# A parallel pooling and attention layer on one core: factoring the first half's norm out of x, and projecting keys and values together

## What is computed

```python
for layer in range(DEPTH):                       # DEPTH = 1, 16 meta frames + 1024 frames, D_MODEL = 2048
    hn = _rmsnorm(h, norm_g[layer])              # each frame divided by its rms, times norm_g
    proj = hn @ w_in[layer]                      # 2048 x 4352
    pv, pg, q, k, v, ag = jnp.split(proj, SPLITS, axis=-1)
    pool_out = _multiscale_pool(pv, pool_w[layer], pool_scale[layer])   # trailing means over 2, 4, 8, 16 frames
    attn_out = _attention_branch(q, k, v, q_norm_g[layer], k_norm_g[layer], sinks[layer])
    mixed = jnp.concatenate([jax.nn.silu(pg) * pool_out, jax.nn.silu(ag) * attn_out], axis=-1)
    h = h + mixed @ w_out[layer]
return h[:, N_META:]
```

## Time and profile before

| | |
|---|---|
| median of 3 runs | 1263.39 us (1261.69 to 1263.98) |
| profiled execution | 1263.45 us, span 1261.8 us |
| TensorE busy | 1239.5 us, 98% of the span |
| VectorE busy | 896.2 us, 71% |
| ScalarE busy | 635.4 us, 50% |
| POOL busy | 68.6 us, 5% |
| HBM read, written | 125.14 MB, 8.39 MB |

### The profile page before, as it was taken

The page is one execution under the profiler, slowest core; times in us unless marked ns, Lnnn a source line. Parts: engine busy times, 40 slices in busy tenths (PEclk is TensorE's granted clock), DMA queues, the critical chain, the costliest instruction groups (busy, mean ns, idle before and its releaser), DMA issues.

```text
span 1261.8 us, 19307 instructions
## 1 busy us (share of the span) xinstructions
PE 1239.5 (98%) x6200; PEld 1042.5 (83%) x6200; DVE 896.2 (71%) x1425; ACT 635.4 (50%) x1490; POOL 68.6 (5%) x78
## 2 busy tenths in 40 slices
PE   4999999999999999999999999999999999999998
PEld 4988898898988987888888888888888888788887
DVE  6557786888879886665644677788798887854553
ACT  6434456465563654544533344655646556444442
POOL 0000000010010110000000000000101103000000
PEclk9999999999999999999999999999999999999999
DMA  5232333222332225544533333222322222343442
GB/s 211 83 92 78 96 96 85 84 77 67 101 92 78 73 67 206 188 137 147 189 126 91 91 94 88 83 82 86 98 72 88 75 92 88 112 133 125 166 142 84
DMA packets 70609, 134.38 MB, mean 106 GB/s; under 512 B 8064, under 2 KB 10240, under 8 KB 69888
## 3 DMA queue, kind: packets, MB, share of 16 engines
q1 hardware_dynamic: 68160, 125.17, 31.6%
q0 software_dynamic: 2384, 8.39, 1.9%
HBM read 125.14 MB, written 8.39 MB: 106 GB/s over the span
## 4 chain that ended last, share of the span: by engine, by line
PE 94%; DVE 3%; DMA 1%; ACT 1%; issue 1%; SPq 0%; ACTq 0%
PE R L1059 19%; PE R L1060 18%; PE R L1063 18%; PE S L1282 4%; PE S L1283 4%; PE S L1281 4%; PE OP L1283 2%; PE OP L1281 2%; PE R L1282 2%; PE OP L1282 2%; PE R L1283 2%; PE R L1281 2%; PE OP L1060 1%; PE OP L1063 1%; PE OP L1059 1%; PE OP L1207 1%
## 5 line engine op out<-in xcount | busy, mean ns | idle before, releaser
L430 ACT ACTIVATE wh<-raw 128x512 fp32r<-128x512 f32 x400 | 250.4, 631 | 494.4 <-PE R L1063 269.8
L725 DVE TENSOR_TENSOR wl<-raw,wh 128x512 fp32r<-128x512 f32 x400 | 282.1, 708 | 241.7 <-ACT wh L430 240.5
L1059 PE MATMUL R<-act_h,wh 128*128 128x512 f32 (+1 forms) x1168 | 426.2, 370 | 0.0
L1060 PE MATMUL R<-act_l,wh 128*128 128x512 f32 (+1 forms) x1168 | 422.5, 367 | 0.0
L1063 PE MATMUL R<-act_h,wl 128*128 128x512 f32 (+1 forms) x1168 | 403.2, 365 | 0.0
L1059 PEld LDWEIGHTS R<-act_h,wh 128*128 128x128 f32 x1168 | 220.1, 188 | 36.9 <-DVE wl L725 0.8
L1060 PEld LDWEIGHTS R<-act_l,wh 128*128 128x128 f32 x1168 | 220.0, 188 | 34.7
L1063 PEld LDWEIGHTS R<-act_h,wl 128*128 128x128 f32 x1168 | 210.5, 188 | 36.8
L949 DVE RECIPROCAL scr<-scr 128x512 f32<-128x512 f32 x32 | 107.3, 3353 | 1.1
L402 POOL TENSOR_TENSOR scr<-scr 128x527 f32<-128x527 f32 (+3 forms) x40 | 50.6, 1265 | 799.2 <-ACT pv_last L430 364.4
L430 ACT ACTIVATE pm<-OP 16x128 fp32r<-16x128 f32 x256 | 68.3, 267 | 5.4
(11 more groups left out here) (206 smaller groups left out, 1825.0 us busy)
## 6 DMA issues: line engine op xcount, KB each, us to landing
raw<-w_in_blocks SPq DMA_DIRECT2D x272, 256.0 KB, 2.6
raw<-w_out_in SPq DMA_DIRECT2D x128, 256.0 KB, 3.0
scr<-xcat SPq DMA_DIRECT2D x32, 256.0 KB, 4.3
mixed<-xcat SPq DMA_DIRECT2D x4, 1024.0 KB, 8.3
res<-xcat SPq DMA_DIRECT2D x16, 256.0 KB, 3.2
out<-scr POOLq DMA_DIRECT2D x14, 256.0 KB, 2.6
out<-res POOLq DMA_DIRECT2D x14, 256.0 KB, 4.9
scr<-pool_w_in SPq DMA_DIRECT2D x8, 256.0 KB, 3.2
```

What stands on the lines that cost most here:

```text
L430: return nc.scalar.activation(dst, src, ACT.Copy)
L725: return nc.vector.tensor_tensor(dst, a, b, ALU.subtract)
L1059: mm(o, wh[:, b, w], act_h[:, k, c], start=(k == 0), stop=False)
L1060: mm(o, wh[:, b, w], act_l[:, k, c], start=False, stop=False)
```

## The change

Half one: x is transposed as it is, and each frame's factor is applied when a product leaves PSUM. For that, the factors are laid out in columns (`r_columns`), transposed by TensorE after query block 0 (`r_transposes`), and copied to a row buffer `rb` that all partitions hold (`r_rows`). All products now leave PSUM through VectorE (`scaled`): times `rb` in half one, times 1.0 in half two. That holds for queries (`q_out`), keys and values (`kv_out`), gates (`gate_in`) and pooled values (`pv_out`, formerly ScalarE's). ScalarE squares queries and keys from SBUF. The gate is now x (1 + tanh(x/2)), with the factor 0.5 put into `o_out` and `hscale` (`gate_tanh`, `gate_out`). The sums of squares of x come after the splits of x, four passes between weight splits. x is loaded in five column pieces, weight blocks between them. Keys and values are projected block by block in turn (`first_tiles`), in both halves. The steps of a query tile move: the copy out stands where the square stood, remainder and sums of squares one step later, root and `q_norm` one step later as well. `QB` and the waits on banks follow.

```diff
-FIRST_SPLITS = {2: 2, 5: 3, 7: 4, 11: 5, 15: 6}
+FIRST_SPLITS = {0: (0,), 3: (1, 2), 7: (3, 4), 11: (5, 6), 15: (7,)}
+FIRST_LOADS = ((0, 2), (2, 4), (4, 8), (8, 12), (12, 16))
...
+        QB = [S[:, 0, :]] + [(R[1][:, :], R[0][:, :], O)[t % 3] for t in range(PAIRS - 1)]
+        YB = [R[0][:, :], S[:, 0, :], S[:, 1, :], O]
...
+            def first_frames(i):
+                k0, k1 = FIRST_LOADS[i]
...
+            def first_block(n, free=True):
+                load_block(n, n % RAW, w_in[TILE_BLKS * (n % 2) + n // 2, :, :], free)
+            sp.dma_start(cst[:, 0:P], consts[:, 0:P]).then_inc(s_id, 16)
+            sp.dma_start(x_meta, xcat[0:META, :]).then_inc(s_xmeta, 16)
+            first_frames(0)
+            sp.dma_start(vec[:, :], vecs).then_inc(s_vec, 16)
+            first_block(0, free=False)
+            first_frames(1)
+            first_block(1, free=False)
+            first_frames(2)
+            first_block(2, free=False)
+            first_block(3, free=False)
+            first_frames(3)
+            sp.dma_start(cst[:, P:C_N], consts[:, P:C_N]).then_inc(s_cst, 16)
+            first_frames(4)
...
-            act.wait_ge(s_init, 5)
-            for n in range(RAW):
-                split_high(0, n)
...
+            def first_stats(r):
+                stats(x_first[r], P, r, r, r)
...
+                for off in FIRST_SPLITS.get(k, ()):
+                    split_high(0, off)
...
+            first_stats(0)
+            first_stats(1)
+            act.wait_ge(s_init, 5)
...
+                for s in range(5 if h == 0 else 0, KV_BLKS):
                     split_high(h4, s + LEAD)
+                    if h == 0 and s < 7:
+                        first_stats(s - 3)
...
+                def r_columns():
+                    act.wait_ge(s_xrs, 2)
+                    for r in range(ROWT):
+                        copy(r_col[:, r, :], xrs[:, r:r + 1].to_broadcast([P, P])).then_inc(s_rc, 1)
+                    copy(r_meta, xrs[0:META, ROWT:ROWT + 1].to_broadcast([META, P])).then_inc(s_rc, 1)
+                def r_rows():
+                    act.wait_ge(s_rt, 1)
+                    copy(rb[:, META:COLS], PT[:, :]).then_inc(s_rb, 1)
+                    copy(rb[:, 0:META], PM[:, 0:META]).then_inc(s_rb, 1)
...
                 def q_square(t):
-                    product_done(act, h, KV_BLKS + t * TILE_BLKS)
+                    act.wait_ge(s_qv, h * PAIRS + t + 1)
                     if t >= 2:
                         act.wait_ge(s_qss, h * PAIRS + t - 1)
                     for dst in (q_sq[t % 2], q_sqh[t % 2]):
-                        nc.scalar.activation(dst, QB[t % 4][:, :], ACT.Square).then_inc(s_qsq, 1)
+                        nc.scalar.activation(dst, mixed[:, PAIRS + t, :], ACT.Square).then_inc(s_qsq, 1)
...
                 for s in range(Q_BLKS + 1):
+                    if s < Q_BLKS:
+                        split_high(h4 + KV_BLKS // RAW, s + LEAD)
+                    if s == 1 and h == 0:
+                        r_rows()
+                    if s == 2:
+                        k_square()
+                    if s == 4:
+                        k_sqrt()
                     if s and s % 4 == 0:
                         q_square(s // 4 - 1)
-                    if s < Q_BLKS:
-                        split_high(h4 + KV_BLKS // RAW, s + LEAD)
-                    if s > 4 and s % 4 == 1:
+                    if s > 4 and s % 4 == 2:
                         q_sqrt(s // 4 - 1)
...
-                    def gate_exp(n, bank):
-                        product_done(act, h, n0 + (0, 4, 16, 20)[n])
...
+                    def gate_tanh(n):
+                        act.wait_ge(s_gv[n], ONE + G + 1)
+                        if n:
+                            act.wait_ge(s_gt[n - 1], ONE + G + 1)
                         else:
-                            act.wait_ge(s_me, ONE + G * 2)
-                        nc.scalar.activation(gate[n], bank[:, :], ACT.Exp, scale=-1.0).then_inc(s_ge[n], 1)
-                    def pv_out(jj):
-                        product_done(act, h, n0 + 8 + 4 * jj)
...
-                        ins.then_inc(s_pve, 1)
+                            act.wait_ge(s_gt[3], ONE + G)
+                        nc.scalar.activation(gate_t, gate[n], ACT.Tanh, scale=0.5).then_inc(s_ge[n], 1)
...
+                def scaled(dst, src, c):
+                    if h == 0:
+                        return nc.vector.tensor_tensor(dst, src, rb[:, c], ALU.mult)
+                    return nc.vector.tensor_scalar(dst, src, 1.0, None, ALU.mult)
...
+                def q_out(t):
+                    product_done(dve, h, KV_BLKS + t * TILE_BLKS)
+                    scaled(mixed[:, PAIRS + t, :], QB[t], slice(META, COLS)).then_inc(s_qv, 1)
                 def q_norm(t):
                     n = h * PAIRS + t
                     dve.wait_ge(s_qsd, n + 1)
                     nc.vector.reciprocal(q_rs[t % 2], q_rs[t % 2]).then_inc(s_qrs, 1)
                     dve.wait_ge(s_qrs, n + 1)
-                    nc.vector.scalar_tensor_tensor(mixed[:, PAIRS + t, :], QB[t % 4][:, :], gq8[:, :],
+                    nc.vector.scalar_tensor_tensor(mixed[:, PAIRS + t, :], mixed[:, PAIRS + t, :], gq8[:, :],
                                                    q_rs[t % 2], ALU.mult, ALU.mult).then_inc(s_qn, 1)
                 for s in range(Q_BLKS + 1):
                     if s and s % 4 == 0:
-                        square_low(s // 4 - 1)
+                        q_out(s // 4 - 1)
                     if s < Q_BLKS:
                         split_low(h4 + KV_BLKS // RAW, s + LEAD)
-                    if s > 4 and s % 4 == 2:
+                    if s == 1:
+                        kv_out()
+                    if s == 2:
+                        k_square_low()
+                    if s == 4:
+                        k_norm()
+                    if s > 4 and s % 4 == 1:
+                        square_low(s // 4 - 1)
+                    if s > 4 and s % 4 == 3:
                         q_norm(s // 4 - 1)
...
-                    def silu(n, bank):
...
+                    def gate_in(n, bank):
+                        product_done(dve, h, n0 + (0, 4, 16, 20)[n])
+                        scaled(gate[n], bank[:, :], slice(META, COLS)).then_inc(s_gv[n], 1)
+                    def gate_out(n):
                         dve.wait_ge(s_ge[n], G + 1)
-                        nc.vector.tensor_scalar(gate[n], gate[n], 1.0, None, ALU.add).then_inc(s_ga, 1)
...
-                        nc.vector.tensor_tensor(gate[n], bank[:, :], gate[n], ALU.mult).then_inc(s_gt[n], 1)
+                        nc.vector.scalar_tensor_tensor(gate[n], gate_t, 1.0, gate[n],
+                                                       ALU.add, ALU.mult).then_inc(s_gt[n], 1)
+                    def pv_out(jj):
+                        product_done(dve, h, n0 + 8 + 4 * jj)
+                        for bank, c in span_banks(h, PVB[h][jj]):
+                            scaled(pv[jj][:, c], bank, c)
...
+                        ins.then_inc(s_pve, 1)
...
+            def first_tiles(h):
+                for n in range(KV_BLKS):
+                    b, banks = n // 2, (KB, VB)[n % 2][h]
+                    pe.wait_ge(s_wl, ONE + h * NBLK + n + 1)
...
+                    for kk in range(4):
+                        k = 4 * b + kk
+                        w = slice(kk * P, (kk + 1) * P)
+                        if h == 0 and n % 2 == 0:
+                            pe.wait_ge(s_xl, k + 2)
...
+                        if kk == 3:
+                            last.then_inc(s_blk, 1)
+                        if h == 0 and n % 2 == 0 and k + 4 < KT:
+                            first_group(k + 4)
...
+                def r_transposes():
+                    pe.wait_ge(s_rc, ROWT + 1)
+                    nc.tensor.transpose(PM[:, 0:META], r_meta, ident[0:META, 0:META])
+                    for r in range(ROWT):
+                        last = nc.tensor.transpose(PT[:, r * P:(r + 1) * P], r_col[:, r, :], ident)
+                    last.then_inc(s_rt, 1)
...
                 def q_events(s):
-                    if s == 0:
+                    if s == 0 and h == 0:
+                        r_transposes()
+                    elif s == 3:
+                        k_squares()
+                    elif s == 8:
                         v_windows()
-                    elif s % 4 == 0:
+                    elif s > 4 and s % 4 == 1:
                         sum_squares(s // 4 - 1)
                 for t in range(PAIRS):
-                    pe.wait_ge(s_qn, QB_FREE + h * PAIRS + t - 3)
-                    if t == 0 and h == 0:
-                        pe.wait_ge(s_kn, 1)
-                    elif t == 1:
+                    if t == 1:
+                        pe.wait_ge(s_ke, SPANS_BY[h + 1])
+                    elif t == 3:
                         pe.wait_ge(s_vT, (3, 4)[h])
-                    elif t == 2:
```

(58 more changed lines are left out.)

274 lines of the change are left out of this document (127 added, 147 removed).

## The result

The changed kernel takes **1320.4 us** (median of 4 runs, 1317.8 to 1322.6) against 1263.1 us for the kernel before on the same chip: ratio 1.0454, 95% interval 1.0441 to 1.0467, slower by 57 us. The prediction was 1296 us with a range up to 1312: the sign was right, the size too small by 24 us, and the time lies outside the range.

The account below looks back on a forecast made before the run. TensorE, busy 98% of the span, was taken as the bound, so only its waits count: 1263.45 - 12.6 + 3.0 + 21.1 + 22.4 - 1.5 = 1295.9, so 1296 us; own range 1280 to 1310, with rival 1 1272 to 1312.

Parts of the forecast that it names:

- The start: Before the first product: four sums of squares and five multiplies removed, first product at 9.8 us; -12.6 us (-14 to -8).
- Norm factors: After the first query block: TensorE waits 2.5 us for norm columns, then transposes for 0.5 us; +3.0 us (+0.5 to +5).
- Query tiles: Sums of squares wait because VectorE's copy out stands behind the previous tile's reciprocal; +21.1 us (+10 to +28).
- Pooling tiles: Second tile waits for the first's copy from shared bank R2, behind unit 0's output in VectorE; 8 x 2.8, +22.4 us.
- Ends: Last gates of each half: quicker gates remove the waits of L1281 and L1076; -1.5 us (0 to -3).
- rival 2: After each of eight pooling waits, TensorE runs at half pace (1.2 GHz clock): 22 us more, 1318 us; chance 0.08.

Follow-up runs that it names:

- experiment 2: Changed kernel with VectorE doing the query norm multiplications one step earlier in each group of four: 1299.9 us, ratio 1.0295 to the kernel before.
- experiment 1: Changed kernel with VectorE copying the pooled values (pv_out(0)) ahead of the attention output (o_out(0)) at step 12: 1294.3 us, ratio 1.0247.
- experiments 1, 3 and 4: 1 has its own line; 3 and 4: changed kernel with twelve, then six unused filler matmuls before each pooling wait: 1311.0 and 1308.6 us.
- experiments 5 to 7: Changed kernel with SBUF places of before; shifted 64 bytes instead of 96; only the output projection's stationary-operand tiles as before: 1312.8, 1317.7, 1313.3 us.
- experiment 5: Changed kernel with row_buf, hscale and res2 moved in SBUF so all other tiles lie as in the kernel before: 1312.8 us, ratio 1.0403.

## Why the prediction was wrong, step by step

- **The start**, forecast -12.6: measured -11.7. First product 10.97 us instead of 9.8 (a 1.01 us wait for a column load). Right.
- **Norm factors**, forecast +3.0: wait 2.4 to 2.5 us and 0.57 us of transposes. Right.
- **Query tiles**, forecast +21.1, by tile 1.0, 0, 1.0, 1.0, 2.5, 1.5, 1.0, 2.55: measured in half one 1.27, 0, 1.02, 1.01, 2.40, 1.15, 1.02, 2.67, both halves 20.7. Right to a few tenths for each tile; experiment 2 shows the cause.
- **Pooling tiles**, forecast 8 x 2.8 = 22.4: measured 4 x 2.4 in half one and 4 x 3.0 in half two, 21.7. Right, and experiment 1 shows the cause. The reason given for half two, a shared bank, was wrong: it is the wait that is shared. The copy of half two takes 686 ns from PSUM with one source, so the 0.69 taken was right. The rule cited there from the Trainium skill (VectorE: DVE Perf Modes, "Why PSUM operands drop a tier") agrees with this trace: 686 ns, where the one-source operation within SBUF took 421 ns.
- **Ends**, forecast -1.5: the waits of L1281 and L1076 are gone, but two of 0.6 us each came at the last unit's `pm` (L1288). About 0; a small miss.
- **The clock**, left out of the sum and priced as rival 2 at 22 us and 0.08. This is the step that failed. It was argued that these waits "are half as long as the 5.4 us seen, and no row shows a fall after less". The kernel before had no wait between 0.6 and 5.4 us, so its trace could say nothing on 2.4 to 3 us, in either direction; the absence of rows was taken for a reason. Nor is the 5.4 us case clear evidence of what a wait does: the kernel after also starts its products at half pace (the second and third are 0.22 us apart at 11.34, and 0.12 us apart from 13.69 on), where its only wait since its first work was 1.0 us. Nine stretches at clock 0.50 cost 14.5 us, and experiments 1, 3 and 4 show that the idleness brings them. Without them the time would have been inside the range: the executions with fillers whose mean clock was 1.000 took 1306.0 and 1306.7 us. The rule cited there from the Trainium skill (TensorE: Matmul & The Clock Gate, Part 1) agrees with this trace: 0.50 at 1007 us, behind 3 us of idleness; four of the thirteen waits were not followed by it. The rival's size was too high: it took 2.75 us for each of eight pooling waits, where six fell, at 1.7 us on average, and forgot the query and norm-column waits.
- **The output projection's pace**, not in the text at all: +5.8 us, from a shift of 96 bytes in a list of allocations that the diff shows in two lines (experiments 5 to 7).

The forecast of 1296 and these two, 14.5 and 5.8, give 1316. Of the 4 us still missing, 2.5 are those not placed and most of the rest are the start and the ends, which gave less than forecast. Rival 2's own figure, 1318 us, lies near the result by luck: it priced the clock 7 us too high and knew nothing of the 5.8 us of the output projection. Even a range that ended at it would have missed 1320.4.

## What to carry to other kernels

A wait that a change puts into TensorE's queue can cost more than its length: where the trace before has no wait of the length forecast, it can't rule out that matmuls behind it run at the 1.2 GHz level, and the range has to take that in (here nine of thirteen waits of 2.4 to 3.0 us, 1.3 to 2.5 us each). A step that is moved to an engine belongs where the other engine asks for it, not behind what the table already had: here three exchanges of order (a few lines each) were worth 26, 20 and 4.5 us. Together with the later transposes, the places of before and the wait that half two doesn't need, they turned a loss of 57 us into a gain of 8. And when a buffer's size changes, look at what lies behind it before comparing two kernels.

## What the runs showed that I had not expected

- The same wait is followed by the half clock in one execution and not in another. In the profiled executions with fillers the waits of 2.66 us of the last query tiles are untouched, yet nothing behind them runs at half pace; in the kernel after both do. With twelve fillers (us, busy of the five engines, granted clock, DMA share, GB/s), behind the wait that ends at 150.9:

```profile
151.00:152.00 1.00, 1.00 (x5) 0.81 (x6) 0.00 (x0) 0.29 (x1) 0.00 (x0) 1.00 0.08 16
```

  and the kernel after, behind the same wait:

```profile
154.00:155.00 1.00, 1.00 (x3) 0.81 (x3) 0.00 (x0) 0.04 (x1) 0.00 (x0) 0.50 0.08 16
```

  The executions of that kernel spread over 7.9 us, with mean clocks of 1.000 (1306.0 us) to 0.995 (1313.9 us), where the kernel before spreads over 2 us. With the places of before (experiment 5) seven of the same thirteen waits were followed by it. What decides it is open.
- A shift of the stationary operands by 64 or 96 bytes a partition slows 512-column matmuls from 229.4 to 232.8 and 233.3 ns.
- The clock need not fall within the idle time. Behind the wait that ends at 1007.8 it does (1.00 at 1005, 0.87 at 1006, 0.50 at 1007), and so behind three others, so that the first matmul already runs at half pace. Behind the other five the matmuls begin at full pace and the clock falls 0.2 to 1.2 us later, as behind the wait that ends at 193.7 (same columns as above):

```profile
193.00:194.00 1.00, 0.30 (x2) 0.33 (x3) 1.00 (x4) 0.00 (x0) 0.32 (x1) 1.00 0.07 27
194.00:195.00 1.00, 1.00 (x8) 1.00 (x7) 0.86 (x3) 0.00 (x0) 1.00 (x1) 0.69 0.00 0
195.00:196.00 1.00, 1.00 (x7) 1.00 (x6) 0.23 (x1) 0.00 (x0) 0.12 (x1) 0.50 0.56 100
```
